# Sixteen roots of a three-block transformer kernel: the power on GpSimd and one Newton step, in place of integer steps and three Newton steps on VectorE

## The reference, cut to what matters

```python
def rms_norm(x, g):
    xf = x.astype(jnp.float32)
    y = xf * lax.rsqrt(jnp.mean(xf * xf, axis=-1, keepdims=True) + RMS_EPS)
    return (y * g.astype(jnp.float32)).astype(x.dtype)

def swiglu(x, wi, wo):
    gate, up = jnp.split(x @ wi, 2, axis=-1)
    return (jax.nn.silu(gate) * up) @ wo
```

## Time and profile before

| | |
|---|---|
| median of 3 runs | 1520.33 us |
| the profiled execution, its own time | 1519.9 us |
| its span in the profile | 1518.1 us |
| TensorE busy, share of the span | 98% |
| VectorE | 58% |
| ScalarE | 47% |
| GpSimd | 6% |
| DMA queue of the weights, share of 16 engines | 52.0% |

### The profile page before, as it was taken

How to read it: one execution, slowest core, us unless ns; L and a number is a source line. 1 busy time by engine, 2 the same in 40 slices (tenths; PEclk the granted TensorE clock), 3 DMA queues, 4 the chain that set the end, 5 groups by cost and what they waited for, 6 DMA issues and landing times.

```text
span 1518.1 us, 16928 instructions
## 1 busy us (share of the span) xinstructions
PE 1486.0 (98%) x7061; PEld 1234.9 (81%) x7061; DVE 876.0 (58%) x1040; ACT 710.2 (47%) x834; POOL 84.6 (6%) x101
## 2 busy tenths in 40 slices
PE   8999999999999999999799999999999889999999
PEld 6888888888888888888688888888888768888887
DVE  6465456565545655459765554755547786765543
ACT  6444345554434444344554444543436666354432
POOL 0000012000000000006000000000000440000000
PEclk9999999999999999999999999999999999999999
DMA  9555472365555655544455556565556342555552
GB/s 315 177 184 177 133 258 98 130 199 189 194 167 194 194 180 188 173 147 153 138 182 193 173 175 207 181 192 183 180 169 207 124 165 86 194 179 189 187 180 70
DMA packets 143890, 265.66 MB, mean 175 GB/s; under 512 B 7070, under 2 KB 24950, under 8 KB 143558
## 3 DMA queue, kind: packets, MB, share of 16 engines
q1 hardware_dynamic: 141974, 259.11, 52.0%
q0 software_dynamic: 1104, 4.35, 0.9%
q10 hardware_dynamic: 736, 1.12, 0.2%
HBM read 263.52 MB, written 1.05 MB: 174 GB/s over the span
## 4 chain that ended last, share of the span: by engine, by line
PE 89%; DVE 7%; ACT 2%; POOL 1%; issue 1%; POOLq 0%; DVEq 0%; ACTq 0%
PE ps L527 28%; PE ps L529 27%; PE ps L528 27%; PE ps L556 2%; DVE wlo L1468 2%; PE ps L539 1%; PE ps L906 1%; POOL m_qf L2088 0%; ACT whi L1082 0%; PE ps L710 0%; PE ps L1042 0%; PE ps L654 0%; DVE d_i L1796 0%; PE ps L620 0%; DVE d_m L1792 0%
## 5 line engine op out<-in xcount | busy, mean ns | idle before, releaser
L1468 DVE TENSOR_TENSOR wlo<-raw,whi 128x2048 fp32r<-128x2048 f32 (+4 forms) x268 | 568.8, 2127 | 434.5 <-ACT whi L1082 434.4
L1082 ACT CAST whi<-raw 128x2048 fp32r<-128x2048 f32 (+4 forms) x268 | 473.5, 1770 | 449.8 <-PE ps L529 449.1
L527 PE MATMUL ps<-whi,xt_hi 128*128 128x512 f32 (+3 forms) x1376 | 535.1, 389 | 5.2 <-DVE wlo L1468 5.2
L529 PE MATMUL ps<-whi,xt_lo 128*128 128x512 f32 (+3 forms) x1376 | 529.1, 385 | 0.0
L528 PE MATMUL ps<-wlo,xt_hi 128*128 128x512 f32 (+3 forms) x1376 | 528.5, 384 | 0.0
L527 PEld LDWEIGHTS ps<-whi,xt_hi 128*128 128x128 f32 x1376 | 259.0, 188 | 56.8 <-issue 4.0
L529 PEld LDWEIGHTS ps<-whi,xt_lo 128*128 128x128 f32 x1376 | 258.9, 188 | 51.4
L528 PEld LDWEIGHTS ps<-wlo,xt_hi 128*128 128x128 f32 x1376 | 259.0, 188 | 48.9
L527 PE MATMUL ps<-whi,yt_hi 128*128 128x512 f32 (+3 forms) x108 | 43.6, 404 | 8.0 <-DVE wlo L1468 6.8
L1108 ACT ACTIVATE junk<-X 128x512 f32<-128x512 f32 x40 | 25.4, 634 | 44.5 <-DVE X L1523 41.1
L529 PE MATMUL ps<-whi,yt_lo 128*128 128x512 f32 (+3 forms) x108 | 42.0, 389 | 0.0
(11 more groups left out here) (381 smaller groups left out, 1586.2 us busy)
## 6 DMA issues: line engine op xcount, KB each, us to landing
raw<-in_ffn_wi SPq DMA_DIRECT2D x79, 1024.0 KB, 5.2
raw<-in_ffn_wo SPq DMA_DIRECT2D x40, 1024.0 KB, 5.0
raw<-in_ffn_w_gate SPq DMA_DIRECT2D x20, 1024.0 KB, 5.1
raw<-in_ffn_w_up SPq DMA_DIRECT2D x20, 1024.0 KB, 5.1
raw<-in_ffn_w_down SPq DMA_DIRECT2D x20, 1024.0 KB, 5.0
raw<-in_w_in SPq DMA_DIRECT2D x14, 1024.0 KB, 5.4
raw<-in_ffn_wi SPq DMA_DIRECT2D x16, 512.0 KB, 4.8
raw<-in_even_w_in SPq DMA_DIRECT2D x8, 1024.0 KB, 5.8
```

The source lines that it names most:

```text
L527: e.matmul(o, h, hi_w, start=i == 0 and j == 0, stop=False)
L529: t = e.matmul(o, l, hi_w, start=False, stop=end and j == nk - 1)
L1082: e.copy(whi[0:n, v % SPLIT, c], raw[0:n, v % RAW, c]).then_inc(s_hi.mark(*[(v, j) for j in js]), 1)
L1468: e.tensor_tensor(wlo[0:n, v % SPLIT, c], raw[0:n, v % RAW, c], whi[0:n, v % SPLIT, c].bitcast(F32), ALU.subtract).then_inc(s_lo.mark(*[(v ...
```

## The change

The root's first value is no longer made of the bit pattern. GpSimd computes it as `nv` to the power of -0.5 (`root`, one TENSOR_TENSOR with the operator pow and a tile `power` that holds -0.5 everywhere, written once at the start), and VectorE waits for it and makes one Newton step of three instructions, the last of which writes the result. `nv`'s last instruction now carries a mark for GpSimd. The calls of `root` are written into GpSimd's order at fixed places: fk's ahead of the forget rows, k's behind the queries' rotation. To make room for `power`, the two spare tiles `kr_room` of the key's rotation now lie in `mat.P1`.

```diff
--- before.py
+++ after.py
@@ -213,6 +213,7 @@
         nv = sb("nv", [128, 32])
         na = sb("na", [128, 32])
         nb = sb("nb", [128, 32])
+        power = sb("power", [128, 32])
         ny = sb("ny", [128, 32])
         RS = sb("RS", [128, 2])
         RF = sb("RF", [128, 2])
@@ -426,9 +427,9 @@
             s24 = sb("m_s", [128, 32], F32, sc)
             r24 = sb("m_r", [128, 32], F32, sc)
             r_lat = sb("m_rl", [128, 6], F32, sc)
-            kr_room = [sb("m_kr1", [128, 32], F32, sc), sb("m_kr2", [128, 32], F32, sc)]
             q_room = [LAT[:, 0, 0:256], LAT[:, 1, 0:256]]
             mat = Attention("m_", lambda n, s: sb(n, s, F32, sc), (FQ[:, :, :].rearrange("p b n -> p (b n)"), FK[:, 0, :]))
+            kr_room = [mat.P1[:, 0, 0:32], mat.P1[:, 0, 32:64]]
         with ExitStack() as sc:
             c2.room(lambda *a: sb(*a, c=sc))
 
@@ -1486,23 +1487,18 @@
                 turned(("xt", x, n), ("xt", x), XT, 4 * n, lambda i: gains_of[x](4 * n + i))
 
             def rsqrt(src, n, scales, dst, name):
+
                 v, a, b, y = nv[:, 0:n], na[:, 0:n], nb[:, 0:n], ny[:, 0:n]
                 q.wait_ge(*norm_done[0])
                 for c, m, s in scales:
-                    e.tensor_scalar(nv[:, c:c + m], src[:, c:c + m], s, EPS, ALU.mult, ALU.add).then_inc(s_dve.mark(), 1)
-                after_mine()
-                e.tensor_scalar(a.bitcast(I32), v.bitcast(I32), 1, None, ALU.logical_shift_right).then_inc(s_dve.mark(), 1)
-                after_mine()
-                e.tensor_scalar(y.bitcast(I32), a.bitcast(I32), -1.0, 1597463007.0, ALU.mult, ALU.add).then_inc(s_dve.mark(), 1)
-                for c in (1.0, 1.0 / 4, 1.0 / 16):
-                    after_mine()
-                    e.tensor_tensor(a, y, y, ALU.mult).then_inc(s_dve.mark(), 1)
-                    after_mine()
-                    e.scalar_tensor_tensor(b, a, c, v, ALU.mult, ALU.mult).then_inc(s_dve.mark(), 1)
-                    after_mine()
-                    e.scalar_tensor_tensor(y, b, 3.0, y, ALU.subtract, ALU.mult).then_inc(s_dve.mark(), 1)
-                after_mine()
-                e.tensor_scalar(dst, y, -1.0 / 8, None, ALU.mult).then_inc(s_dve.mark(name), 1)
+                    e.tensor_scalar(nv[:, c:c + m], src[:, c:c + m], s, EPS, ALU.mult, ALU.add).then_inc(
+                        s_dve.mark(*([("mean", name)] if c + m == n else [])), 1)
+                q.wait_ge(*s_pool["root", name])
+                e.tensor_tensor(a, y, y, ALU.mult).then_inc(s_dve.mark(), 1)
+                after_mine()
+                e.scalar_tensor_tensor(b, a, -0.5, v, ALU.mult, ALU.mult).then_inc(s_dve.mark(), 1)
+                after_mine()
+                e.scalar_tensor_tensor(dst, b, 1.5, y, ALU.add, ALU.mult).then_inc(s_dve.mark(name), 1)
                 norm_done[0] = s_dve.now()
 
             def row_scale(x, dst, name):
@@ -2023,12 +2019,19 @@
                 after_mine()
                 e.tensor_tensor(x, a, b, ALU.add).then_inc(s_pool.mark(name), 1)
 
+            def root(name, n):
+                q.wait_ge(*s_dve["mean", name])
+                after_mine()
+                e.tensor_tensor(ny[:, 0:n], nv[:, 0:n], power[:, 0:n], ALU.pow).then_inc(s_pool.mark(("root", name)), 1)
+
             def phase_done(f):
                 q.wait_ge(*s_mm[f.d[1].at[5], 1])
                 q.wait_ge(*s_act["sq", f.name, 1, 1])
                 q.wait_ge(*s_dve["rs", f.name])
 
             def gla():
+                root(("rs", "in"), 2)
+                root(("rs", "a1"), 2)
                 phase_done(a1)
                 e.dma_start(masks[:, :], T["c_masks"]).then_inc(s_mix.mark(), 16)
                 e.dma_start(win0[:, :, :], T["c_win0"].rearrange("p (g t) -> p g t", g=4)).then_inc(s_mix.mark(), 16)
@@ -2054,8 +2057,12 @@
                     e.tensor_tensor(kv[:, :, 0:s], kt[:, :, 0:s], ev[:, :, 0:s], ALU.mult).then_inc(s_pool.mark(("kx", lv)), 1)
                     q.wait_ge(*s_act["ex", lv, 1])
                     e.tensor_tensor(qx, qt[:, :, s:2 * s], ev[:, :, s:2 * s], ALU.mult).then_inc(s_pool.mark(("qx", lv)), 1)
+                root("r8", 8)
+                root(("rs", "gla"), 2)
 
             def dsa():
+                root(("rs", "a2"), 2)
+                root(("rs", "b1"), 2)
                 q.wait_ge(*s_act["dk"])
                 for tt in range(2):
                     rotate(dK[:, tt, :].rearrange("p (h b f) -> p h b f", h=2, b=2), 2, 0, 1, 64, room2, tt, ("dk", tt))
@@ -2066,6 +2073,9 @@
                 rotate(dQ[:, 1, 512:1024].rearrange("p (h b f) -> p h b f", h=4, b=2), 4, 0, 1, 64, room2, 1, ("dq", 1))
 
             def mla():
+                root("rf", 2)
+                root("rs_fin", 2)
+                root(("rs", "c1"), 2)
                 phase_done(c1)
                 e.dma_start(fc[:, :], T["c_forget"]).then_inc(s_gate.mark(), 16)
                 e.dma_start(rope_gain[:, 0, :], T["mla_q_rope_gain_2"][0].partition_broadcast(128)).then_inc(s_gate.mark(), 16)
@@ -2082,13 +2092,16 @@
 
                 def head_norm(name):
                     views = norm_views[name]
+                    root(("hnr", name), 8 * len(views))
                     q.wait_ge(*s_dve["hnr", name])
                     for i, x in enumerate(views):
                         after_mine()
                         t = e.tensor_tensor(x, x, r24[:, 8 * i:8 * i + 8].unsqueeze(2).broadcast_to([128, 8, x.shape[2]]), ALU.mult)
                         t.then_inc(s_pool.mark(*([("hn", name)] if i == len(views) - 1 else [])), 1)
 
+                root(("rs", "lat"), 6)
                 head_norm("fq")
+                root(("hnr", "fk"), 16)
                 q.wait_ge(*s_dve["c"])
                 q.wait_ge(*s_gate["all"])
                 c = C[64:80, 1, :]
@@ -2106,12 +2119,15 @@
                     q.wait_ge(*s_dve["kr", 1])
                     rotate(x.rearrange("p h (b f) -> p h b f", b=2), 8, 64, 1, 16, q_room, tt, ("qrope", tt))
                 head_norm("k")
-
+                root(("rs", "mla"), 2)
+
+            e.memset(power[:, :], -0.5).then_inc(s_pool.mark("power"), 1)
             e.dma_start(pos_i[0:2, :], T["positions"].rearrange("a (t p) -> (a t) p", p=128)).then_inc(s_pos.mark(), 16)
             e.dma_start(pos_i[2:4, :], T["positions_2"].rearrange("a (t p) -> (a t) p", p=128)).then_inc(s_pos.mark(), 16)
             e.dma_start(inv[:, :], T["c_inv"]).then_inc(s_pos.mark("all"), 16)
             gla()
             dsa()
+            root(("rs", "dsa"), 2)
             q.wait_ge(*s_mm[d_out[1].at[1], 1])
             q.wait_ge(*s_act["sq", "dsa", 1, 1])
             q.wait_ge(*s_dve["rs", "dsa"])
```

## The result

The changed kernel takes 1541.07 us (median of 4 runs, 1538.62 to 1541.45) where the kernel before takes 1520.23 beside it: a ratio of 1.0134, interval 1.0116 to 1.0151. It is **slower by 20.8 us** (1.3%), outside the forecast range. Single executions of one kernel can lie some 2.2 us above its others (of 25 of the kernel before, two took 1522.3 and 1522.6 us and all others 1519.4 to 1520.9), and in the traced ones that did the granted clock between 200 and 240 us was 0.91 where it was 0.96 in most.

The account below looks back on a forecast made before the run. TensorE bounds the kernel, busy 1486.0 of 1518.1 us, so only its waits can change. The terms -1.9 and -3.1 plus powers of 4.6 gave -0.4 us, so 1519.9 us, range 1516.0 to 1532.

Parts of the forecast that it names:

- the price of the power: GpSimd's time for one power, shown by no row: taken as 0.8, 0.9 and 1.1 us at 6, 16 and 32 columns.
- the sum: All gains and losses in `mla`: -5.0 + P(6) + 3P(16) + P(32), P(n) being the power of n columns; -0.4 us.
- both ends: Prices at 6, 16, 32 columns: one pass, 0.12, 0.14, 0.17 us; or twelve passes, 1.5, 1.7, 2.1 us.
- the far end: Each of the five powers in `mla` as dear as the longest GpSimd row there, 3.40 us: 17.0 together, sum +12.
- the fox scores: First place in `mla`: TensorE's scores, waiting for GpSimd's forget rows, gain 1.9 - P(6) - 2P(16) us.
- q and k: Second place in `mla`: TensorE reaches the transposes of k earlier by 3.1 - P(16) - P(32) us.
- The forget rows: GpSimd's sixteen rows behind fk's power start at 1184.1 + P(6) + 2P(16), with a second meeting costing another 2.3 us.
- the guessed 7: VectorE idle ahead of k's first Newton step for the whole of the rotations' rest, some 7 us.
- Rival C: Slower, 1523.4 to 1532 us: a dear power in line five times in `mla`, prices from 8.0 us in sum; chance 0.33.
- rival B: Faster, 1514 to 1517 us: the power is a pass like the others, -4.3, or -6.6 without second meeting; chance 0.27.
- ten row scales and `r8`: Eleven roots outside the latents and head norms: nothing on TensorE waits for them, so their powers cost nothing.
- The expected fall of the wait for `wlo`: TensorE's wait for VectorE's `wlo` at the third block after the latents falls from 5.2 to about 2.2 us.

Follow-up runs that it names:

- e5: The changed kernel with addresses as before and only the roots of q and k taking the power from GpSimd: 1524.58 us against 1519.82.
- e9: The changed kernel with addresses as before and a GpSimd product by 0.01 in place of the power (not the root's value): 1520.79 us against 1520.16.
- e2: The changed kernel with `power` in the room of scratch tile `nb`, so all addresses behind are as before: 1533.27 us against 1520.11.
- e1: The kernel before with only an unused tile of 128 bytes a partition where the change puts `power`: 1529.40 us against 1520.11.
- e4: The changed kernel with addresses as before and only the roots of the latents, fq and fk on GpSimd: 1528.25 us against 1520.11.
- e3: The changed kernel with addresses as before and only the eleven roots outside `mla` on GpSimd: 1519.73 us against 1520.11.
- e8: The changed kernel with addresses as before and k's power moved ahead of the queries' rotation: 1534.99 us against 1519.82.
- e12: The kernel before with an unused 320 bytes a partition ahead of the first feed-forward's own tiles alone: 1519.3 us against 1520.16.

## Why the prediction was wrong

**The step that failed first is the price of the power**: "I take the middle of these, 0.8, 0.9 and 1.1 us". It measured 1.35, 2.90 and 5.43, together 15.5 us in the sum for the 4.6 put down. The middle between a pass like any other and twelve passes wasn't near any row; both ends took a pass to be mostly a fixed time, when of the 2.90 us at 16 columns 2.5 go with the columns. The estimate by the Trainium skill (GPSIMD Engine Reference, "7. Performance pitfalls for Q7 kernels"), 40 ns a column, was short by a factor of four; the rows decide against using that rule for this operator. That the far end, 3.40 us for each of the five, comes near in sum (17.0 for 15.5) is luck: it is the time of a forget row that met VectorE's splits, and at 6 and at 32 columns it is wrong by 2 us each way. With the right prices alone the sum gives 1520.3 + 10.5 = 1530.8: slower, but inside the range. What put the time outside it are the two terms below, about 9.3 and 1.7; all three make 21.5 for the measured 20.8.

**At the measured prices the formula around them was right.** With them the fox scores should lose 1.35 + 5.80 - 1.9 = 5.25, measured 4.64; q and k 8.33 - 3.1 = 5.23, measured 5.28, and 4.8 in e5. The forget rows were to start at 1184.1 + 7.15 + 5.57 of entry shift = 1196.8, and did at 1196.64. They met VectorE's splits twice, 3.40 and 2.47 us against 0.55 for their like, the second of these new. This is what the Trainium skill (Perfetto Trace Analysis, "Optimizing Scalar/DVE Operations") warns of, and the trace agrees. k's two products ran free, 2.16 us, and VectorE idled 9.0 us ahead of k's root, the guessed 7 plus P(16)'s excess of 2.0. The new wait on the fox scores was given as about 3 us and is 2.9. The handovers took 0.09 us from VectorE to GpSimd, as taken, and 0.03 back. At a small price the formula is 5.1 us off (e9), mostly by the clock.

**Rival C had the mechanism**, slower because a dear power stands in line five times in `mla`; its condition, a sum of prices of about 8.0 us or more, is met by 15.5, and the 1530.8 lies inside its 1523.4 to 1532. e2, which is the change without its address effect, measured 1533.3. C had nothing on the addresses. The prediction's own test, "if the power takes over 1.6 or under 0.3 us at 16 columns", catches it with 2.90. C's chance of 0.33 was too small for a price of which nothing was known.

**A term was missing: the addresses.** The sum has no term for the diff's new tile and what it moves. It is +8.8 us by the steps, +9.3 in e1, and nearly half of the loss. The test "if TensorE stalls anywhere outside `mla` that it didn't before" wouldn't even have caught it, since nothing stalls: what shows it is TensorE's busy time at an equal count of matmuls.

**A second term was missing: the clock behind a stall.** The sum counted a stall by its length. Measured are 1.7 us on top of it in the change, 2.8 in e2, 3.4 in e4 and 3.85 in e9, with a mean of 0.50 to 0.59 granted in the stretches read behind it. Mainly for this reason rival B would have failed even with its own condition met: e9 has a cheap operator and gains nothing.

**What was costed at nothing held**: ten row scales and `r8` (e3, -0.4), the busy time taken off VectorE, and VectorE's wait for k's power behind the rotations (e8). The expected fall of the wait for `wlo` to 2.2 us fell with the price: two powers at 2.90 and one at 1.35 are more than the 5.57 us saved, so it grew to 5.9.

No version tried beats the kernel before beyond what a measurement can tell; the best medians are e12's and e3's.

## What to carry to other kernels

An operator that no row shows should be measured at two widths before it is put on a path; one width doesn't tell a fixed time from a price per column. Before moving work off a busy engine, ask what then stands in line on the other one, in its fixed order, and whether the stall at the consumer goes away or only moves: a few microseconds won in one place can be lost at a wait of nearly the same length a little later, with a slower TensorE behind it. When a kernel grows slower at an equal count of matmuls and without a new wait, look at the step from matmul to matmul and at where the operands lie, since any new small tile moves all that are allocated behind it.

## What the runs showed of the hardware that was not expected

- A power on GpSimd costs 0.39 us and 157 ns a column (128 partitions, float32): 0.70 at 2, 5.43 at 32 columns. A product there costs 0.19 to 0.25 us at 2 to 32 columns.
- The step of TensorE's 512-column matmuls depends on the start of the stationary operand by its remainder by 256 bytes: 226.8 ns at 128, 229.0 at 64, 232.4 to 232.9 at 0, 233.3 at 192. Why, and whether other shapes do the same, wasn't tried. That this operand is the one that counts is inferred: the other operands of these matmuls, `whi` and `wlo`, lie ahead of all that was moved, e12 moves the first stage's tiles alone and changes that stage's step alone, and the `xt` blocks, whose operand didn't move, kept 227.1 to 227.2 ns.
- Behind stalls of TensorE of 2.9 to 5.9 us the products or the block that followed had a mean granted clock of 0.50 to 0.59, all or mostly the 1.2 GHz level: in e4 and e9 (4.0 and 5.9 us) eight score products took 3.78 us against 1.89; in the change (2.9 us) the six matmuls of the next block stood mostly 0.43 us apart where it is 0.23 at the full clock. Behind 1.25 us in e9 it stayed at 1.00.
- A GpSimd row of 16 x 256 that takes 0.55 us took 2.47 and 2.67 us where it met one split of VectorE, and 3.40 where it met several back to back.
